# Moving a few waits in a two-layer decoder step: operand pieces, a silu, a modulated chunk, sums of squares and decode transposes

## The reference, cut to what matters

```python
for i in range(DEPTH):                       # DEPTH = 2
    sh1, sc1, g1, sh2, sc2, g2 = modulation(c)
    h = rmsnorm(x, norm_mix_pre[i]) * (1 + sc1) + sh1
    if i % 2 == 0:  o = (b_gate * causal_dwconv(c_gate * v, prev, conv_w)) @ w_out   # short conv
    else:           o = mla_mixer(h, ...)                                             # latent attention
    x = x + g1 * rmsnorm(o, norm_mix_post[i])
    h = rmsnorm(x, norm_ffn_pre[i]) * (1 + sc2) + sh2
    a, v = jnp.split(h @ w_in, 2, axis=-1)                                            # 1024 -> 2 x 2816
    a = causal_dwconv(a, prev, conv_w)
    o = (jax.nn.silu(a + conv_b) * v) @ w_out                                         # 2816 -> 1024
    x = x + g2 * rmsnorm(o, norm_ffn_post[i])
```

## Time and profile before

| | us |
|---|---|
| median of three runs | 2526.23 |
| lowest, highest | 2520.61, 2527.99 |
| the profiled execution | 2528.15 |
| its span in the trace | 2526.4 |
| PE busy in it | 2414.9 (96%) |
| DVE busy | 1686.2 (67%) |
| ACT busy | 956.3 (38%) |
| POOL busy | 229.8 (9%) |

### The profile page before, as it was taken

How to read it: one execution, slowest core, us unless ns; L and a number is a source line. 1 busy time by engine, 2 the same in 40 slices (tenths; PEclk the granted TensorE clock), 3 DMA queues, 4 the chain that set the end, 5 groups by cost and what they waited for, 6 DMA issues and landing times. The chain is left out here.

```text
span 2526.4 us, 44971 instructions
## 1 busy us (share of the span) xinstructions
PE 2414.9 (96%) x18990; PEld 2287.1 (91%) x18990; DVE 1686.2 (67%) x2619; ACT 956.3 (38%) x1668; POOL 229.8 (9%) x319
## 2 busy tenths in 40 slices
PE   7999999999999999999999999779999999999998
PEld 5888999989999999999975888559989999999998
DVE  5422236797777777787465666976797777777773
ACT  4211114543333334554434665024543333334542
POOL 1000000001111010000002000210001111010001
PEclk8999999999999999999999999999999999999999
DMA  9677333237876657666010032872337876757654
GB/s 343 228 267 262 102 92 119 101 122 156 200 187 168 151 178 240 200 214 188 18 34 22 22 148 110 332 259 103 101 121 156 197 188 169 153 175 249 201 180 129
DMA packets 345162, 415.84 MB, mean 165 GB/s; under 512 B 16909, under 2 KB 287890, under 8 KB 332861
## 3 DMA queue, kind: packets, MB, share of 16 engines
q0 software_dynamic: 54320, 213.24, 28.2%
q1 hardware_dynamic: 290641, 199.72, 25.8%
HBM read 358.48 MB, written 118.08 MB: 189 GB/s over the span
## 5 line engine op out<-in xcount | busy, mean ns | idle before, releaser
L2851 PE MATMUL ps<-h_hi,w_hi 128*128 128x344 f32 x816 | 263.7, 323 | 0.8 <-ACT a_sb L1491 0.8
L2853 PE MATMUL ps<-h_hi,w_lo 128*128 128x344 f32 x816 | 260.4, 319 | 0.0
L2852 PE MATMUL ps<-h_lo,w_hi 128*128 128x344 f32 x816 | 260.3, 319 | 0.0
L1806 DVE TENSOR_TENSOR d_lo<-d_raw,d_hi 128x768 fp32r<-128x768 f32 (+2 forms) x176 | 154.1, 886 | 88.5 <-ACT d_hi L1198 87.7
L1198 ACT ACTIVATE d_hi<-d_raw 128x768 fp32r<-128x768 f32 (+2 forms) x176 | 136.5, 787 | 137.8 <-DMA d_raw<-in_ffn_w_out 70.2
L1538 ACT ACTIVATE op_hi_Y<-op_raw_Y 128x512 fp32r<-128x512 f32 x80 | 50.5, 632 | 311.8 <-DVE op_raw_Y L2357 162.0
L2851 PEld LDWEIGHTS ps<-h_hi,w_hi 128*128 128x128 f32 x816 | 153.5, 188 | 5.4 <-issue 4.3
L2853 PEld LDWEIGHTS ps<-h_hi,w_lo 128*128 128x128 f32 x816 | 153.3, 188 | 0.0
L2852 PEld LDWEIGHTS ps<-h_lo,w_hi 128*128 128x128 f32 x816 | 153.2, 188 | 0.0
L1009 POOL DMA_DIRECT2D act_d<-g_sb x52 | 41.2, 792 | 1026.2 <-DVE g_sb L2387 652.2
L3140 PE MATMUL ps<-h_hi,op_hi_X 128*128 128x258 f32 x640 | 129.7, 284 | 2.6 <-DVE op_lo_X L2338 2.6
(11 more groups left out here) (523 smaller groups left out, 7192.8 us busy)
## 6 DMA issues: line engine op xcount, KB each, us to landing
wsum_d<-in_ffn_w_out POOLq DMA_DIRECT2D x88, 704.0 KB, 10.8
mod_late<-in_mod_w SPq DMA_DIRECT2D x40, 1024.0 KB, 9.9
fr<-in_ffn_w_in SPq DMA_DIRECT2D x80, 512.0 KB, 5.1
d_raw<-in_ffn_w_out SPq DMA_DIRECT2D x72, 384.0 KB, 3.5
act_d<-g_sb POOLq DMA_DIRECT2D x52, 516.0 KB, 5.8
xc<-x_d POOLq DMA_DIRECT2D x10, 1376.0 KB, 6.5
w_raw<-in_sc_w_in SPq DMA_DIRECT2D x24, 512.0 KB, 3.7
d_raw<-wsum_d SPq DMA_DIRECT2D x32, 384.0 KB, 3.3
```

The lines of the kernel that those rows point to most:

```text
L1806: dve.tensor_tensor(w_lo[k.slot][:, 0:k.kt, :], w_raw[k.slot][:, 0:k.kt, :], w_hi[k.slot][:, 0:k.kt, :].bitcast(F32), ALU.subtract).then_i ...
L2851: pe.matmul(o, w_hi[k.slot][:, t, :], h_hi[:, t, up_cols(c)], start=t == 0, stop=False)
L2852: pe.matmul(o, w_hi[k.slot][:, t, :], h_lo[:, t, up_cols(c)], start=False, stop=False)
L2853: ins = pe.matmul(o, w_lo[k.slot][:, t, :], h_hi[:, t, up_cols(c)], start=False, stop=t == KD - 1)
```

## The change

No instruction is added or removed on any engine; the lists of SP and POOL are the same. Five things are moved, two of them together.

1. `HI_AT` and `LO_AT`: the pieces Xa and Xb of the third product are split one tile later on ACT; on DVE Xa stands behind the split of block b+16 and a sum of squares. In d = 1 and d = 3.
2. `up()`: ACT splits weight block b+3 before the last silu, and DVE before the last gate. Twice.
3. `down22(1)` alone: the last chunk is modulated into `o_sb`, not in place in `xc`; the wait for the store of `xc` moves from before the modulation to before the last `h_lo`; the sums of squares stand before a weight split (`w_lo`), not behind it.
4. `ahead()` for d = 0 and 2: `x_sums` after k-tile 4 of the part before, `x_roots` after k-tile 0; each four k-tiles earlier.
5. Decode: the transposes `keys_turn(1)` stand before a wait for ACT's copies of the attention output; the first `decode_top` stands before the transpose of kTr.

```diff
--- before.py
+++ after.py
@@ -1400,7 +1400,7 @@
                 act.activation(y_tok[yt % 4][0:n, 0:4, :], bank((0, 3)[yt % 2])[0:n, :].rearrange("p (k n) -> p k n", k=4),
                                ACT.Copy).then_inc(yt_ea, 1)
 
-            HI_AT = {1: (2,), 4: (3,), 5: (4,), 8: (5,), 9: (6,), 12: (7,), 13: (8,), 16: (9,), 17: (10,), 20: (11,), 21: (12,),
+            HI_AT = {1: (2,), 5: (3,), 6: (4,), 8: (5,), 9: (6,), 12: (7,), 13: (8,), 16: (9,), 17: (10,), 20: (11,), 21: (12,),
                      22: (13,), 24: (14,), 25: (15,)}
 
             def down22(d):
@@ -1470,7 +1470,7 @@
                         square_x(j0 + 2, m, xc, sqx)
                     root(q_post(d, 2) + 1)
                     for m in range(KD):
-                        h_round(j0 + 2, m, xc, B)
+                        h_round(j0 + 2, m, o_sb, B)
                 else:
                     for i, (t0, n) in enumerate(y_tiles(2)[0:3]):
                         act.wait_ge(yt_mm, 2 * yt + i + 1)
@@ -1591,8 +1591,8 @@
                 hi_to(b_down + 1)
                 piece_hi(d, 1)
                 hi_to(b_down + 2)
+                hi_to(b_down + 3)
                 silu(KF - 1)
-                hi_to(b_down + 3)
                 gate_hi(stage, KF - 1, oa_hi["Yb"][:, KF - 1 - KEPT, :])
 
             up(0)
@@ -1939,17 +1939,19 @@
                     elif tile_sem is not None:
                         ins.then_inc(tile_sem, 1)
 
-            def last_h(d, A, B):
+            def last_h(d, A, B, u):
 
                 j = NU * (d + 2) - 1
                 rs = bank(7)[:, 0:UC]
-                modulate_s(j, xc, xc, A, B, rs)
+                modulate_s(j, xc, u, A, B, rs)
                 for m in range(KD + 1):
                     if m < KD:
-                        dve.scalar_tensor_tensor(xc[:, m, 0:PL], xc[:, m, 0:PL], A[:, m, 0:1], rs[:, 0:PL], ALU.mult, ALU.mult
+                        dve.scalar_tensor_tensor(u[:, m, 0:PL], xc[:, m, 0:PL], A[:, m, 0:1], rs[:, 0:PL], ALU.mult, ALU.mult
                                                  ).then_inc(u_ready, 1)
+                    if m == KD and u is not xc:
+                        x_stored(d, 2)
                     if m:
-                        h_low(j, xc, B, [m - 1], hk_ready)
+                        h_low(j, u, B, [m - 1], hk_ready)
 
             def scale_o(d, c, G):
 
@@ -2061,7 +2063,7 @@
                 lo_to(b + KD + 3)
                 rs_in(q_post(d, 2) + 1)
                 x_stored(d, 2)
-                last_h(d, A, B)
+                last_h(d, A, B, xc)
 
             def y_out_tile(yt, n):
                 dve.wait_ge(yt_mm, 2 * yt + 2)
@@ -2124,7 +2126,7 @@
                 dve.wait_ge(so_added, 7 * NU * d + n - 1)
                 dve.tensor_tensor(dst[:], (sqd[0] if s in (1, 5) else dst)[:], sqd[s % 2][:], ALU.add).then_inc(so_added, 1)
 
-            LO_AT = {5: (3,), 6: (4,), 9: (5,), 10: (6,), 13: (7,), 14: (8,), 17: (9,), 18: (10,), 21: (11,), 22: (12,),
+            LO_AT = {6: (4,), 9: (5,), 10: (6,), 13: (7,), 14: (8,), 17: (9,), 18: (10,), 21: (11,), 22: (12,),
                      23: (13,), 25: (14,), 26: (15,)}
             SUM_MID = {3: (0, 1), 4: (1, 1), 5: (2, 1), 12: (3, 1)}
             SUM_END = {2: (0, 0), 3: (1, 0), 4: (2, 0), 11: (3, 0)}
@@ -2151,6 +2153,8 @@
                         tails_out(KF, t0, range(0, 4))
                     if t in SUM_MID:
                         stage_sum(d, *SUM_MID[t])
+                    if t == 6:
+                        piece_lo(d, 3)
                     lo_to(i0 + 5)
                     if t == 2:
                         tails_out(KF, t0, range(4, 6))
@@ -2220,12 +2224,11 @@
                 scale_o(d, 2, G)
                 scale_tiles(d, 2, G, range(KD))
                 if more:
+                    add_last(j0 + 2)
                     lo_to(i0 + 6)
-                    add_last(j0 + 2)
                     inv_root(q_post(d, 2) + 1)
                     rs_in(q_post(d, 2) + 1)
-                    x_stored(d, 2)
-                    last_h(d, A, B)
+                    last_h(d, A, B, o_sb)
                 else:
                     for i, (t0, n) in enumerate(y_tiles(2)[0:3]):
                         dve.wait_ge(yt_mm, 2 * yt + 3 + i + 1)
@@ -2464,8 +2467,8 @@
                 lo_to(b_down + 2)
                 second_half(NF - 1)
                 last_part(NF - 1)
+                lo_to(b_down + 3)
                 gate_f(NF - 1)
-                lo_to(b_down + 3)
                 dve.wait_ge(g_ready, UP0[stage] + KF)
                 settle()
                 dve.sem_inc(tail_ready, 1)
@@ -2626,8 +2629,10 @@
                 dve.wait_ge(pg_in[s], 32 * (m // 6 + 1))
                 wait(dve, sc_mm, m - 1)
                 dve.transpose(kT[z][:, 0:n].rearrange("p t c -> p (t c)"), pg[s][:, 0:n].rearrange("p t c -> p (t c)"))
+                if among == 0:
+                    decode_top(among)
                 dve.transpose(kTr[z][:].rearrange("p t c -> p (t c)"), pgr[m % 5][:].rearrange("p t c -> p (t c)"))
-                if among is not None:
+                if among:
                     decode_top(among)
                 dve.transpose(kT[z][:, n:].rearrange("p t c -> p (t c)"), pg[s][:, n:].rearrange("p t c -> p (t c)")
                               ).then_inc(kt_d, 1)
@@ -2652,8 +2657,8 @@
             dve.wait_ge(e_ready, UNITS)
             dve.wait_ge(p_t_e, turn_items(UNITS))
             dve.wait_ge(pv_mm, 4 * H)
+            keys_turn(1)
             dve.wait_ge(pv_e, 4 * H)
-            keys_turn(1)
             step(dve.memset(ps[:, 6:8, 0:KR], 0.0))
             step(dve.tensor_reduce(sel[:], ident[:].rearrange("p (g w) -> p w g", w=32)[:, 0:H, :], AX.X, ALU.add))
             eye = ident[0:NS, 0:NS]
@@ -3091,8 +3096,8 @@
                     up_part(v, 1, [0])
                     up_part(v, 1, [1])
                     pe.wait_ge(a_e, AE0[f"f{d // 2}"] + 1)
-                    up_part(a2, 0, [0])
-                    up_part(a2, 0, [1], {0: x_sums, 4: x_roots})
+                    up_part(a2, 0, [0], {4: x_sums})
+                    up_part(a2, 0, [1], {0: x_roots})
                 pair_tiles(a, v, NU - 1, (KD - 1) * (NU + d), h + 2)
 
             b = first["sc"]
```

## The result

| | before | changed |
|---|---|---|
| first comparison, median | 2527.11 | 2511.57 (2509.80 to 2513.01, 4 runs) |
| ratio, 95% interval | | 0.9943 (0.9923 to 0.9963) |
| second comparison, median | 2526.58 | 2516.14 (2513.73 to 2521.64, 6 runs) |
| ratio, 95% interval | | 0.9962 (0.9950 to 0.9974) |
| profiled execution | 2528.15 | 2513.01 |

What follows compares the result with a forecast made beforehand. PE bounds the kernel, busy 2414.9 us of a 2526.4 us span, so only its waits or low clock matter. 3.7 + 2.8 + 3.8 + 0.3 + 0 = 10.6 us off 2526.23 gives 2515.6, range 2506 to 2524.

Steps and rivals of the forecast that it cites:

- Earlier sums: Starts of the d = 0 and 2 stages: PE's 1.47 us waits go; 3.7 us together (2.9 to 3.8).
- Last chunk: End of down22(1): the modulation, no longer waiting for the store, comes 2.8 us earlier (1.2 to 3.7).
- Block b+3 and the third product in layer 0: Narrowing product, d = 1, to tile 9: items 2 and 1 gain 5.4 us, 3.8 after the clock charge.
- The new wait before tile 8: d = 1: PE waits 2.3 us for the third product where it did not wait before.
- The step that failed: d = 1: item 2's 2.7 us earlier start of tile 2 carried on in full to tile 9.
- The chain before tile 8: Both layers: on ACT Xa's high half follows b+15 (load 8.3 and 10.7 us), then b+16; then Xa's low half on DVE.
- The same in layer 1: Narrowing product, d = 3, to tile 9: items 2 and 1 gain 1.9 us, 0.3 after the clock charge.
- The forecast wait of 3.1: d = 3, before tile 8: PE waits 3.1 us for Xa's low half.
- The low clock: Behind the new wait before tile 8: one low-clock stretch of 1.55 to 1.6 us charged in each layer.
- The rule of the Trainium skill: PE's clock: throttled by default, released by activity, so each new wait costs a low stretch; no size given.
- Decode: Decode: ACT's exponential waits 13.15 us, last for a DMA no edit moves; gain 0, bounds -2 and +1.
- Sum: Whole kernel: 10.6 us less, 2515.6 from a median of 2526.23, 0.42% faster; chance 0.49.

Runs made afterwards that it cites:

- e10: Item 1 alone on the kernel before: 2518.36 us against 2523.92, ratio 0.9982 (0.9972 to 0.9993).
- e9: Item 5 alone on the kernel before: 2524.38 us against 2523.92, ratio 1.0004 (0.9996 to 1.0013).
- the six named at e4: The six executions with items 1 and 2 as changed: the changed kernel twice, e1, e2, e7 and e8, at 2511.57 to 2516.99 us.
- e4: The changed kernel without item 1: 2517.29 us, ratio to before 0.9970 (0.9959 to 0.9982).
- e8: The changed kernel without item 4: 2513.98 us, ratio to before 0.9965 (0.9951 to 0.9979).
- e6: The changed kernel without item 2: 2517.85 us, ratio to before 0.9965 (0.9952 to 0.9978).
- e7: The changed kernel without item 3: 2516.99 us, ratio to before 0.9965 (0.9952 to 0.9978).
- e1: The changed kernel without item 5: 2513.95 us, ratio to before 0.9956 (0.9943 to 0.9969).
- e2: The changed kernel with only keys_turn(1) put back behind the wait for ACT's copies: 2515.28 us, ratio to before 0.9956 (0.9943 to 0.9969).
- e3: The changed kernel with Xa's low half again before block b+16's split on DVE: 2519.03 us, ratio to before 0.9971 (0.9961 to 0.9981).
- e5: e3 with the sum of squares ss_d also before Xa's low half on DVE: 2510.66 us, ratio to before 0.9940 (0.9927 to 0.9952).
- e11: e5 with Xa's high half before block b+15 on ACT, not behind it: 2507.86 us, ratio to before 0.9938 (0.9924 to 0.9952).

## Why the prediction was right, point by point

**Earlier sums (3.7).** 1.85 us were forecast for each place. S1 gave 1.87, in every kernel. In d = 2, S6 is 146.5 on average without the item (145.75, 146.51, 147.07, 146.74) and 144.5 with it (143.91 to 145.47), 2.0.

**Last chunk (2.8).** The trace gave 2.4 in S3 in the profiled pair, the mean over all kernels 1.7, within the bounds. The chain went as worked out: the sums came back with no wait, and the modulation waited 1.45 us for PE's spread, for which I had allowed 1.2 with no row to show it, and for no DMA. DVE's timeline of the changed kernel:

```profile
1186.90 0.15 DVE L1875 TENSOR_SCALAR root_t<-ps 86x4 f32<-86x4 f32 x1
...
1189.53 0.23 DVE L1908 TENSOR_TENSOR tmp_s<-xc,modv 128x64 f32<-128x64 f32 x1 [1.45 <-PE ps L2729]
```

What the forecast took for fixed was the landing of the store: 3.06 us of wait in one trace, 2.11 and 1.79 in others, none in e10.

**Block b+3 and the third product in layer 0 (5.4, 3.8 with the clock).** S2 is shorter by 4.6 in the pair, and by 4.6 if the mean of the two kernels without items 1 and 2 (before and e9, 471.7) is set against that of the six named at e4 (467.2). The new wait before tile 8 was forecast at 2.3 and measured at 2.11, 1.06, 1.80, 2.02, 2.21 and, in e8, 1.64. How it splits between the items was wrong. 2.7 us were given to item 2, and by e6 and e10 its gain in layer 0 is gone by tile 9 when item 1 is there. (Without item 1, e4 against before and e9, it gives 1.7.) 1.55 of the 2.7 was the low clock behind b+3, which in layer 0 only the trace of before has: PE waited 1.72, 1.70 and 1.06 us there in e6, e9 and e10, with the full clock behind it. The step that failed is the one that shifted all times behind tile 2 by 2.7 us, the load of b+15 and Xa with them. That they are readier when PE comes later is my reading of the two traces.

The chain before tile 8 was partly another one too, so that its length came out right is in part luck. I had Xa's high half behind the load of b+15. In layer 0 of the changed kernel b+15 landed in 6.5 us, not 8.3, and the low half of Xa waited behind b+16 on DVE. In layer 1 it was as worked out: b+15 landed 9.2 us after its issue, ACT had idled 6.02 us for it, and Xa, b+16 and Xa's low half followed without a gap on ACT. ACT's timeline of the changed kernel:

```profile
2283.88 0.74 ACT L1198 ACTIVATE d_hi<-d_raw 128x640 fp32r<-128x640 f32 x1 [6.02 <-DMA d_raw<-in_ffn_w_out]
2284.53 1.91 ACT L1323 ACTIVATE oa_hi_Xa<-hh 128x2064 fp32r<-128x2064 f32 x1
2286.52 0.84 ACT L1198 ACTIVATE d_hi<-d_raw 128x768 fp32r<-128x768 f32 x1
```

The same layer in the second execution of the changed kernel shows another load. Block b+15 had landed 3.4 us after its issue and ACT did not wait for it; ACT waited 2.76 us for b+16, which landed 9.4 us after its issue, and PE waited 2.91 us before tile 8:

```profile
2288.40 0.85 ACT L1198 ACTIVATE d_hi<-d_raw 128x768 fp32r<-128x768 f32 x1 [2.76 <-DMA d_raw<-wsum_d]
```

In ten of the twelve layers of the six executions ACT waited like this for b+16's load, 0.41 to 3.25 us, behind Xa's high half; in four of the ten it had waited over 3 us for b+15 too. Only in two (layer 1 of the changed kernel and of e7) was b+15 the last late load, as forecast. So the forecast named the right tile and the right piece, and mostly the wrong load.

**The same in layer 1 (1.9, 0.3 with the clock).** S7 is shorter by 2.2 in the pair, by 1.8 on the means (470.4 of before and e9, 468.7 of the six). Here item 2 carries it: without it S7 is 471.95 (e6) and 472.57 (e10), and item 1 by itself gives nothing. The forecast wait of 3.1 was 2.82, and 1.94 to 3.41 in the others. The low clock, which I charged in each layer, came in neither.

**The low clock.** This is the mis-sized term. I charged 3.2 us over both layers as certain. Over the twelve layers of changed, changed again, e1, e2, e7 and e8 it came behind tile 8's wait in four (e2, layer 0; e1, e7 and e8, layer 1), each time for some 1.5 us: the tile took 6.7 to 6.8 us and not 5.27. At that rate the term is 1.0. The two layers without it would give 7.3, less 1.0 is 6.3, and 6.4 were measured on the means. The rule of the Trainium skill that speaks against item 1 (page "TensorE: Matmul & The Clock Gate", section "What's actually happening") told the direction, not the number: eight of the twelve waits, 1.06 to 2.91 us long, cost no clock.

**Decode (0).** Right by e9 and e1, though the first trace seemed to contradict it with 5 us. Had I stopped at the pair of traces, I would have written a mechanism for it.

**Sum.** On the means: 3.9 + 1.7 + 4.6 + 1.8 = 12.0 us, where 10.6 were forecast and 15.5 and 10.4 timed. The total was near for a reason that is partly luck: the last chunk came 1.1 us short, and the low clock, charged 2.2 us too high, more than made up for it.

## What to carry to other kernels

A wait on an engine's list is worth what stands behind it: moving one instruction past a late load helps only if the next in the chain (here a two-buffer square, freed by an add that nobody looks at) moves with it; e3 and e5 differ in that alone, with medians of 2519.03 and 2510.66. Before explaining a gain found by comparing two traces, look at how long the same stretch takes in other executions; of the eight segments here, S1 repeats to 0.02 us and S5 only to 5. Where a piece is late, ask on both of its engines for the load that it is queued behind.

## What the runs showed of the hardware that was not expected

Whether the clock falls behind a wait of PE does not follow from the length of that wait in these traces. In e2 PE waited 2.02 us before tile 8 in layer 0 and 2.85 in layer 1. The windows of tile 8 read:

```profile
974.90:981.70 6.80, 6.77 (x34) 6.80 (x35) 5.48 (x6) 3.50 (x6) 0.00 (x0) 0.76 0.30 89
2293.70:2298.90 5.20, 5.20 (x33) 5.19 (x34) 5.07 (x6) 3.44 (x6) 0.00 (x0) 1.00 0.23 67
```

The shorter wait had the low clock, the longer had not. And e9 had 3.06 us before tile 7 in both layers and full clock behind both, where before and e4 had 2.84 to 3.07 and the low clock each time. e9's two windows of tile 7:

```profile
972.50:978.20 5.70, 5.45 (x34) 5.22 (x34) 5.70 (x5) 2.62 (x3) 0.00 (x0) 1.00 0.77 272
2293.70:2299.40 5.70, 5.46 (x34) 5.23 (x34) 5.70 (x5) 2.58 (x3) 0.00 (x0) 1.00 0.69 250
```

What decides it was not found. A fall behind the wait before tile 8 costs some 1.5 us (a tile of 6.8 us for 5.27). Behind the wait before tile 7, which takes 5.64 us in e9, it costs 0.9 to 2.4 (6.58 us in layer 0 of before, 8.01 in layer 1 of e4). That it is part of the scatter between executions is likely and was not measured; e11, which waits 0.6 us before tile 8, has a narrow spread of times, 2.0 us over five runs.
